# Dilated attention: q and k sorted by class for each dilation, v single-buffered and reloaded by dilation, 16 staging slots

## The chip, the cores and the metric

The kernel runs on one core of a Trainium2 chip. The metric is the device time of a run in microseconds (us); smaller is better.

## What is computed

The program is a transformer block of 2048 tokens and width 1024 with two kinds of attention, followed by a second, sliding-window block. The change lies in one stage alone, the dilated attention of the first block: 8 heads of 64, each token attending in a radius of 64 positions at three dilations. Cut from the reference:

```python
DIL_HEADS = 8
DIL_PATTERNS = ((128, 1), (512, 4), (2048, 16))
...
def dilated_branch(q, k, v, slopes, window, dilation):
    r = window // (2 * dilation)
    ...
    qs = split(q)              # positions split into residue classes
    kw = window3(split(k))     # each block of r with its two neighbours
    vw = window3(split(v))
    ...
    s = jnp.einsum('bnqche,bnkche->bnchqk', qs, kw).astype(jnp.float32) * scale + bias
    s = jnp.where(mask, s, MASK_VALUE)
    m = jnp.max(s, axis=-1, keepdims=True)
    e = jnp.exp(s - m)
    l = jnp.sum(e, axis=-1, keepdims=True)
    o = jnp.einsum('bnchqk,bnkche->bnqche', e.astype(v.dtype), vw)
```

For dilation d the tokens t with equal t mod d form a class; within it the pattern is a plain band of radius 64. The three outputs are merged in a later stage by their softmax sums.

## The kernel before

`build` runs seven stages one after the other: an input projection (names with p_), a global attention (d_), the dilated attention (l_), a merge with a projection (m_), a gated embedding (g_), a second projection (s_), and windowed attention with its projection (w_). Each stage is a `Phase`: it owns its buffers and semaphores, its engines meet at a barrier at the end, and then GpSimd clears the stage's semaphores one by one (L78) before its own work in the next stage.

`dilated_attention` treats 4 pairs of heads. A pair is 24 steps, 8 for each of the dilations 1, 4 and 16, in this order (a dilation is called a level below); a step is two units, a unit 128 queries of one class for the two heads of the pair. Step n on each engine:

- TensorE, `scores`: two bias matmuls (L1110) and then twelve of 64x128 weights (q) and 64x256 keys (L1123), in three passes over the high and low parts of q and k. q and k lie in token order, so at dilation d both operands are read with a distance of d elements: `q_part[own, par, start:start + d * (P - 1) + 1:d]`. At dilation 16 a window holds the whole class and half of the scores are used. Then `transposes` (L1134) of the step before and `values` (L1149) of the one before that, unit by unit; at dilation 16 these are half as many.
- VectorE, `top`: the row maxima (L1071), one TENSOR_REDUCE a step, written into the staging ring; then `move` (L1079, three of four units) and `move_out` (L1084, the outputs into the ring).
- ScalarE, `exp` (L1009), and `move` for every fourth unit (L1018).
- SyncE (SP), the DMA queue, in program order: it waits until a step is staged and issues its two stores (L956). The ring `stage` has 8 slots, so `top` of step n waits until the stores of step n - 4 have landed. At step 2 and 4 of a pair it loads q and k of the next pair into `raw` (L919), at step 6 all of its v, in front of step 6's stores: `if at == 6: load_v(pair + 1)`, 16 DMAs (L933 to L940) into the other half of the double buffer `v`, once in the order of each dilation, 3 MB in all.
- GpSimd: at the start an iota, the zero edges of k and the masks (L976); then for each next pair the high part (L990) and the low part (L992) of q and k.

At the stage's start VectorE zeroes the edges of v (L1035, L1036, 20 memsets), makes distances (L1039, L1043), ScalarE and VectorE split q and k of the first pair, GpSimd cuts the masks out of the distances, and VectorE copies them into `tables` (L1057, L1059), which the first bias matmul needs.

Of the kernel before, what the change touches and what calls it, by code (L numbers as in the profile page):

```python
# [16 lines left out]
ALU = mybir.AluOpType  # L17
ACT = mybir.ActivationFunctionType
F32 = mybir.dt.float32
# [808 lines left out]
def dilated_attention(nc, c, cols, rows, o_parts):  # L828
# [32 lines left out]
    with Phase(nc, "l") as ph:  # L861
        ident = c["ident"]
        raw = ph.sb("raw", [P, 2, S])
        q_hi = ph.sb("q_hi", [P, 2, S], F32R)
        q_lo = ph.sb("q_lo", [P, 2, S], F32R)
        k_hi = ph.sb("k_hi", [P, 2, S + 2 * PAD], F32R)
        k_lo = ph.sb("k_lo", [P, 2, S + 2 * PAD], F32R)
        v = ph.sb("v", [P, 2, CHUNKS, 2 * HD])
# [5 lines left out]
        stage = ph.sb("stage", [P, 8, PAIR_OUT])  # L874
# [5 lines left out]
        v_loaded = ph.sems("v_loaded", 2)  # L880
# [3 lines left out]
        parts_made = ph.sem("parts_made")  # L884
        counted = ph.sem("counted")
# [13 lines left out]
        stored = ph.sems("stored", 8)  # L899
# [15 lines left out]
        def _(sp):  # L915
# [5 lines left out]
            def load_v(pair):  # L921
                if pair >= 2:
                    sp.wait_ge(valued, 2 * SPP * (pair - 1))
                if pair == 0:
                    sp.wait_ge(v_padded, 20)
                at = BV * P + pair * 2 * HD
                src, dst, arrived = rows[:, at:at + 2 * HD], v[:, pair % 2], v_loaded[pair % 2]
                chunk = 0
                for d in (1, 4):
                    tiles = NT // d  # L930
                    for cls in range(d):
                        own = src.rearrange("(i d) n -> d i n", d=d)[cls]
                        sp.dma_start(dst[REACH:P, chunk], own[0:REACH, :]).then_inc(arrived, 16)  # L933
                        sp.dma_start(dst[:, chunk + 1:chunk + tiles],
                                     own[REACH:REACH + (tiles - 1) * P, :].rearrange("(j p) n -> p j n", p=P))\
                          .then_inc(arrived, 16)
                        sp.dma_start(dst[0:REACH, chunk + tiles], own[tiles * P - REACH:tiles * P, :])\
                          .then_inc(arrived, 16)
                        chunk += tiles + 1
                sp.dma_start(dst[:, chunk:chunk + NT], src.rearrange("(i d) n -> i d n", d=NT)).then_inc(arrived, 16)  # L940
# [1323 lines left out]
```

## Time and profile before

| | us |
|---|---|
| median of 3 runs | 3359.24 |
| lowest, highest | 3358.46, 3363.28 |
| the profiled execution's own time | 3359.32 |
| its span, first to last instruction | 3357.2 |
| TensorE busy in the span | 3115.7 (93%) |
| VectorE busy | 1657.7 (49%) |
| ScalarE busy | 1227.4 (37%) |
| GpSimd busy | 454.0 (14%) |

The busy times are means over seven stages with different limits; what the change is worth is read from the l_ stage alone. A row of a trace gives start, duration, engine, line, operation and buffers, and in brackets how long the engine was idle before it and what ended the idle time. Start times are counted from the span's start.

### The profile page before, as it was taken

The page shows a single profiled execution, that of the slowest core. Times are in us where ns is not written, and L with a number is a line of the kernel's source. Part 1 is how long each engine was busy: PE and PEld are TensorE (multiplying, and loading weights), DVE is VectorE, ACT ScalarE, POOL GpSimd, SP SyncE. Part 2 cuts the span into 40 slices and gives each one's busy share as a digit, 9 for nine tenths or more (in the row PEclk, how much of TensorE's full clock was granted, in tenths as well). Part 3 has the DMA queues.
Part 4 walks back from the last instruction along what each step waited for, and adds up shares of the span by engine and source line. Part 5 has one row for each costly group of instructions (what it writes and reads, how often), then busy time and mean ns, then how long its engine had stood idle before and what let it go on. Part 6 is the DMA issues. An engine that isn't in the chain of part 4 may idle for free. (4 is left out here: it accounts for less than half of the span.)

```text
span 3357.2 us, 49168 instructions
## 1 busy us (share of the span) xinstructions
PE 3115.7 (93%) x19138; PEld 2656.3 (79%) x19138; DVE 1657.7 (49%) x2855; ACT 1227.4 (37%) x2695; POOL 454.0 (14%) x249
## 2 busy tenths in 40 slices
PE   7999999997999999879999599699689999799998
PEld 7877778985788888768888478588588888699997
DVE  4466664002888888745445477333341100166664
ACT  3222221011677777635445211222231111254543
POOL 1110110111102101021010344200101100121111
PEclk9999999998999999979899799899899999799999
DMA  5111212223101111042131466422234431444342
GB/s 170 60 66 56 68 61 66 72 63 90 25 22 51 33 33 28 33 120 79 48 92 33 147 225 228 139 73 83 107 121 111 115 100 53 149 141 131 119 127 76
DMA packets 254561, 303.01 MB, mean 90 GB/s; under 512 B 18768, under 2 KB 201088, under 8 KB 251136
## 3 DMA queue, kind: packets, MB, share of 16 engines
q1 hardware_dynamic: 254336, 299.92, 28.7%
q8 instruction: 152, 2.49, 0.3%
q14 instruction: 73, 0.60, 0.1%
HBM read 190.38 MB, written 109.47 MB: 89 GB/s over the span
## 5 line engine op out<-in xcount | busy, mean ns | idle before, releaser
L708 DVE CUSTOM_DVE_ANT_0 d_e<-d_score,d_dist,d_slope 128x1024 f32<-128x1024 f32 x256 | 318.5, 1281 | 64.5 <-PE d_score L764 64.4
L477 PE MATMUL p_acc<-p_h_hi,p_w_hi 128*128 128x512 f32 x768 | 324.2, 422 | 1.0 <-issue 1.0
L477 PE MATMUL p_acc<-p_h_hi,p_w_lo 128*128 128x512 f32 x768 | 300.0, 391 | 0.0
L477 PE MATMUL p_acc<-p_h_lo,p_w_hi 128*128 128x512 f32 x768 | 299.4, 390 | 0.0
L420 DVE RECIPROCAL p_root<-p_root 128x512 f32<-128x512 f32 x64 | 214.6, 3353 | 149.9 <-ACT p_root L344 149.9
L642 ACT ACTIVATE d_e<-d_e,d_neg_top 128x2048 f32<-128x2048 f32 x128 | 257.1, 2008 | 84.8 <-DVE d_neg_top L717 84.6
L787 PE MATMUL d_out<-d_v,d_w_t 128*128 128x128 f32 x2048 | 252.2, 277 | 0.0
L787 PEld LDWEIGHTS d_out<-d_v,d_w_t 128*128 128x128 f32 x2048 | 241.5, 194 | 0.0
L477 PE MATMUL s_acc<-s_h_hi,s_w_hi 128*128 128x512 f32 x576 | 224.4, 390 | 0.0
L477 PE MATMUL s_acc<-s_h_lo,s_w_hi 128*128 128x512 f32 x576 | 224.1, 389 | 0.0
L477 PE MATMUL s_acc<-s_h_hi,s_w_lo 128*128 128x512 f32 x576 | 224.1, 389 | 0.0
L1009 ACT ACTIVATE l_e<-l_score,l_stage 128x256 f32<-128x256 f32 (+1 forms) x384 | 163.3, 437 | 160.1 <-DVE l_stage L1071 157.8
L1071 DVE TENSOR_REDUCE l_stage<-l_score 128x4 f32<-128x1024 f32 (+1 forms) x96 | 100.5, 1047 | 160.0 <-PE l_score L1123 135.8
L477 PEld LDWEIGHTS p_acc<-p_h_hi,p_w_hi 128*128 128x128 f32 x768 | 144.2, 188 | 43.9 <-issue 16.2
L477 PEld LDWEIGHTS p_acc<-p_h_lo,p_w_hi 128*128 128x128 f32 x768 | 144.2, 188 | 43.3 <-issue 14.9
L1149 PE MATMUL l_out<-l_v,l_e_t 128*128 128x64 f32 x1280 | 170.6, 274 | 0.0
L477 PEld LDWEIGHTS p_acc<-p_h_hi,p_w_lo 128*128 128x128 f32 x768 | 144.2, 188 | 30.6
L649 ACT ACTIVATE d_w_t<-d_turn 128x512 f32<-128x512 f32 x256 | 138.9, 597 | 74.8 <-PE d_turn L774 74.8
L1149 PEld LDWEIGHTS l_out<-l_v,l_e_t 128*128 128x128 f32 x1280 | 165.4, 199 | 0.0
L309 POOL TENSOR_TENSOR p_w_lo<-p_w_raw,p_w_hi 128x2048 fp32r<-128x2048 f32 x16 | 73.3, 4584 | 650.6 <-ACT p_w_hi L337 650.6
L732 DVE SCALAR_TENSOR_TENSOR d_e<-d_e,d_ratio 128x2048 f32<-128x2048 f32 x64 | 159.5, 2492 | 0.0
L470 PE MATMUL p_acc<-p_w_hi,p_h_hi 128*128 128x256 f32 x512 | 147.4, 288 | 11.5 <-DVE p_h_lo L390 11.5
(258 smaller groups left out, 6961.4 us busy)
## 6 DMA issues: line engine op xcount, KB each, us to landing
p_w_raw<-in_w_in SPq DMA_DIRECT2D x16, 1024.0 KB, 6.7
cols<-p_stage SPq DMA_DIRECT2D x64, 256.0 KB, 2.3
q<-s_parts SPq DMA_DIRECT2D x128, 128.0 KB, 2.4
w_q<-q SPq DMA_DIRECT2D x16, 1024.0 KB, 8.8
o_parts<-l_stage SPq DMA_DIRECT2D x192, 66.0 KB, 1.7
m_o<-o_parts SPq DMA_DIRECT2D x48, 264.0 KB, 4.9
s_w_raw<-in_a_w_in SPq DMA_DIRECT2D x10, 1024.0 KB, 5.4
rows<-p_stage SPq DMA_DIRECT2D x32, 256.0 KB, 2.1
```

Source lines behind the costliest of these rows:

```text
L309: pool.tensor_tensor(w_lo[:, i % 2], w_raw[:, i % 2], w_hi[:, i % 2].bitcast(F32), ALU.subtract).then_inc(w_lo_made, 1)
L420: dve.reciprocal(root[:, m % 2], root[:, m % 2]).then_inc(root_inverted, 1)
L470: mm = pe.matmul(acc[:, room, two * BLK:(two + 1) * BLK], h_part[:, kt, at], w_part[:, j, kt], start=(kt == 0 and m == 0), stop=(kt == KT ...
L477: mm = pe.matmul(acc[:, room], w_part[:, j, kt, ct * P:(ct + 1) * P], h_part[:, kt, tc * BANK:(tc + 1) * BANK], start=(kt == 0 and m == 0) ...
L642: act.activation(e[:, m % 3, s], e[:, m % 3, s], ACT.Exp, bias=neg_top[:, m % 2, s:s + 1], accum_out=sums).then_inc(exped, 1)
L649: act.activation(w_t[:, m % 2, 4 * r:4 * r + 4], turn[:, r % 2].rearrange("p (b n) -> p b n", n=P), ACT.Copy).then_inc(moved, 1)
L708: dve.tensor_tensor_reduce(e[:, m % 3, s, half * HALF:(half + 1) * HALF], score[:, 2 * half:2 * half + 2].rearrange("p a b -> p (a b)"), d ...
L732: dve.scalar_tensor_tensor(out=e[:, m % 3, 0], in0=e[:, m % 3, 1], scalar=ratio[:, m % 2, 1:2], in1=e[:, m % 3, 0], op0=ALU.mult, op1=ALU. ...
L787: mm = pe.matmul(out[:, m % 2, 0:VW], w_t[:, m % 2, kt], v[:, h % 2, kt], start=(kt == 0), stop=(kt == NT - 1))
L1009: act.activation(e[:, u % 4, h, 0:width(n)], score[:, 2 * (n % 2) + h, scores_of(n, j)], ACT.Exp, bias=stage[:, u % 8, 2 * HD + h:2 * HD + ...
L1071: dve.tensor_reduce(stage[:, 2 * n % 8:2 * n % 8 + 2, 2 * HD:2 * HD + 2], own, AX_X, ALU.max, negate=True)\
L1149: mm = pe.matmul(out[:, n % 2, (2 * j + h) * HD:(2 * j + h + 1) * HD], e_t[:, u % 4, w * h + k], v[:, pair % 2, chunk + k, h * HD:(h + 1) ...
```

## The change

- q and k are kept three times, once for each level, in buffers q_hi1, q_hi4, q_hi16 and so on, each sorted by class, so that all operands of the scores are contiguous. The buffers are single: there is no half for the next pair. The split on GpSimd (or, for the first pair, on ScalarE and VectorE) fills level 1; GpSimd then copies it into the order of level 4 and of level 16, four copies each (`sort_parts`), reading with a distance of 4 or 16 elements. A level's buffers are refilled when the pair before has made its last scores of that level.
- v is single as well, with a buffer for each level (v1, v4, v16). Its 16 loads for the next pair are spread over steps 9 to 11 (v1), 16 to 23 and, in the next pair, 0 to 3 (v4), and 4 (v16), one a step, behind the step's stores. The values wait for v once a level instead of once a pair.
- The staging ring has 16 slots. The stage has 11 semaphores more: `stored` 16 instead of 8, `v_loaded` 3 instead of 2, and two `sorted_made`.
- The loads of raw q and k stand behind the stores of their step. VectorE zeroes 10 edges of v instead of 20; GpSimd's zero edges of k are 8 memsets instead of 4, of fewer elements.

```diff
     STEPS = dilated_steps()
     SPP = len(STEPS)
     TOTAL = PAIRS * SPP
-    PAD = REACH * 4
     WIN = 2 * P
-    CHUNKS = (NT + 1) + 4 * (NT // 4 + 1) + NT
-    V_DMAS = 3 + 4 * 3 + 1
+    LEVELS = len(DILATIONS)
+    SPL = SPP // LEVELS
+    KEYS = (S + 2 * REACH, S + 4 * 2 * REACH, S)
+    CHUNKS = (NT + 1, 4 * (NT // 4 + 1), NT)
+    V_DMAS = (3, 12, 1)
     KINDS = 6
+    SLOTS = 16
+
+    def level_of(n):
+
+        return n % SPP // SPL
+
+    def whole(tensor, d):
+
+        return tensor.rearrange("p (i c) -> p c i", c=d)
+
+    def classes(tensor, d):
+
+        return tensor.rearrange("p (c i) -> p c i", c=d)
+
+    def inner(keys, d):
+
+        return classes(keys, d)[:, :, REACH:REACH + S // d] if d < NT else classes(keys, d)
...
-        q_hi = ph.sb("q_hi", [P, 2, S], F32R)
-        q_lo = ph.sb("q_lo", [P, 2, S], F32R)
-        k_hi = ph.sb("k_hi", [P, 2, S + 2 * PAD], F32R)
-        k_lo = ph.sb("k_lo", [P, 2, S + 2 * PAD], F32R)
-        v = ph.sb("v", [P, 2, CHUNKS, 2 * HD])
+        q_hi = [ph.sb(f"q_hi{d}", [P, S], F32R) for d in DILATIONS]
+        q_lo = [ph.sb(f"q_lo{d}", [P, S], F32R) for d in DILATIONS]
+        k_hi = [ph.sb(f"k_hi{d}", [P, n], F32R) for d, n in zip(DILATIONS, KEYS)]
+        k_lo = [ph.sb(f"k_lo{d}", [P, n], F32R) for d, n in zip(DILATIONS, KEYS)]
+        v = [ph.sb(f"v{d}", [P, n, 2 * HD]) for d, n in zip(DILATIONS, CHUNKS)]
...
-        stage = ph.sb("stage", [P, 8, PAIR_OUT])
+        stage = ph.sb("stage", [P, SLOTS, PAIR_OUT])
...
-            def load_v(pair):
-                if pair >= 2:
-                    sp.wait_ge(valued, 2 * SPP * (pair - 1))
-                if pair == 0:
-                    sp.wait_ge(v_padded, 20)
+            def load_v(pair, level, part):
...
+                if pair >= 1:
+                    sp.wait_ge(valued, 2 * (SPP * (pair - 1) + SPL * (level + 1)))
...
-                sp.dma_start(dst[:, chunk:chunk + NT], src.rearrange("(i d) n -> i d n", d=NT)).then_inc(arrived, 16)
+                src, dst, arrived = rows[:, at:at + 2 * HD], v[level], v_loaded[level]
+                if d == NT:
+                    sp.dma_start(dst[:, :], src.rearrange("(i d) n -> i d n", d=NT)).then_inc(arrived, 16)
+                    return
+                own = src.rearrange("(i d) n -> d i n", d=d)[cls]
+                chunk = cls * (tiles + 1)
+                if part % 3 == 0:
+                    sp.dma_start(dst[REACH:P, chunk], own[0:REACH, :]).then_inc(arrived, 16)
+                elif part % 3 == 1:
+                    sp.dma_start(dst[:, chunk + 1:chunk + tiles],
+                                 own[REACH:REACH + (tiles - 1) * P, :].rearrange("(j p) n -> p j n", p=P))\
+                      .then_inc(arrived, 16)
+                else:
+                    sp.dma_start(dst[0:REACH, chunk + tiles], own[tiles * P - REACH:tiles * P, :])\
+                      .then_inc(arrived, 16)
 
             for item in range(2):
                 load_raw(0, item)
-            load_v(0)
+            sp.wait_ge(v_padded, 10)
+            for level in range(LEVELS):
+                for part in range(V_DMAS[level]):
+                    load_v(0, level, part)
...
-                if pair + 1 < PAIRS:
-                    if at in (2, 4):
-                        load_raw(pair + 1, at // 2 - 1)
-                    if at == 6:
-                        load_v(pair + 1)
                 sp.wait_ge(staged, n + 1)
...
-                    sp.dma_start(own[b * P:(b + 1) * P, :], stage[:, u % 8]).then_inc(stored[u % 8], 16)
-            for s in range(8):
-                sp.wait_ge(stored[s], 16 * 2 * TOTAL // 8)
+                    sp.dma_start(own[b * P:(b + 1) * P, :], stage[:, u % SLOTS]).then_inc(stored[u % SLOTS], 16)
+                if pair + 1 < PAIRS:
+                    if at in (2, 4):
+                        load_raw(pair + 1, at // 2 - 1)
+                    if SPL + 1 <= at < SPL + 4:
+                        load_v(pair + 1, 0, at - SPL - 1)
+                    if at >= 2 * SPL:
+                        load_v(pair + 1, 1, at - 2 * SPL)
+                if pair >= 1:
+                    if at < 4:
+                        load_v(pair, 1, SPL + at)
+                    if at == 4:
+                        load_v(pair, 2, 0)
...
-            for part in (k_hi, k_lo):
-                for edge in (slice(0, PAD), slice(PAD + S, S + 2 * PAD)):
-                    pool.memset(part[:, :, edge].bitcast(F32), 0.0).then_inc(padded, 1)
+            for level, d in enumerate(DILATIONS[:2]):
+                for part in (k_hi[level], k_lo[level]):
+                    length = S // d + REACH
+                    for edge in (slice(0, REACH), slice(length, length + REACH)):
+                        pool.memset(classes(part, d)[:, :, edge].bitcast(F32), 0.0).then_inc(padded, 1)
...
+            def sort_parts(pair, level):
+                d = DILATIONS[level]
+                pool.wait_ge(parts_made, 2 * pair + 2)
+                if pair >= 1:
+                    pool.wait_ge(scored, SPP * (pair - 1) + SPL * (level + 1))
+                for part, out_part in ((q_hi, classes(q_hi[level], d)), (q_lo, classes(q_lo[level], d)),
+                                       (k_hi, inner(k_hi[level], d)), (k_lo, inner(k_lo[level], d))):
+                    own = part[0][:, :] if part in (q_hi, q_lo) else part[0][:, REACH:REACH + S]
+                    pool.tensor_copy(out_part, whole(own, d)).then_inc(sorted_made[level - 1], 1)
+
+            for pair in range(PAIRS):
+                if pair >= 1:
+                    for item, (hi, lo) in enumerate(((q_hi[0][:, :], q_lo[0][:, :]),
+                                                     (k_hi[0][:, REACH:REACH + S], k_lo[0][:, REACH:REACH + S]))):
+                        pool.wait_ge(raw_loaded[item], 16 * (pair + 1))
+                        pool.wait_ge(sorted_made[1], 4 * pair)
+                        pool.wait_ge(scored, SPP * (pair - 1) + SPL)
+                        pool.tensor_copy(hi, raw[:, item]).then_inc(hi_made, 1)
+                        pool.wait_ge(hi_made, 2 * pair + item + 1)
+                        pool.tensor_tensor(lo, raw[:, item], hi.bitcast(F32), ALU.subtract).then_inc(parts_made, 1)
+                for level in (1, 2):
+                    sort_parts(pair, level)
 
...
-                hi = (q_hi[:, 0], k_hi[:, 0, PAD:PAD + S])[item]
-                lo = (q_lo[:, 0], k_lo[:, 0, PAD:PAD + S])[item]
+                hi = (q_hi[0][:, :], k_hi[0][:, REACH:REACH + S])[item]
+                lo = (q_lo[0][:, :], k_lo[0][:, REACH:REACH + S])[item]
...
             def scores(n):
-                pair = n // SPP
-                par, banks = pair % 2, 2 * (n % 2)
+                pair, level, banks = n // SPP, level_of(n), 2 * (n % 2)
                 if n % SPP == 0:
                     pe.wait_ge(parts_made, 2 * pair + 2)
+                elif n % SPL == 0:
+                    pe.wait_ge(sorted_made[level - 1], 4 * pair + 4)
...
                     for j, (d, cls, b, _) in enumerate(step_of(n)):
-                        start = cls + d * P * b
+                        length = S // d + (2 * REACH if d < NT else 0)
                         for h in range(2):
                             own = slice(h * HD, (h + 1) * HD)
-                            q = q_part[own, par, start:start + d * (P - 1) + 1:d]
-                            if d == NT:
-                                keys = k_part[own, par, PAD:PAD + S].rearrange("p (k c) -> p c k", c=NT)\
-                                    [:, cls // 2 * 2:cls // 2 * 2 + 2]
-                            else:
-                                at = PAD + start - d * REACH
-                                keys = k_part[own, par, at:at + d * (WIN - 1) + 1:d]
+                            q = q_part[level][own, cls * (S // d) + b * P:cls * (S // d) + (b + 1) * P]
+                            at = cls * length + b * P if d < NT else cls // 2 * WIN
+                            keys = k_part[level][own, at:at + WIN]
...
+                if n % SPL == 0 and j == 0:
+                    pe.wait_ge(v_loaded[level], 16 * V_DMAS[level] * (pair + 1))
                 wait_moved(pe, u)
...
+                                       v[level][:, chunk + k, h * HD:(h + 1) * HD], start=(k == 0), stop=(k == w - 1))
                 mm.then_inc(valued, 1)
```

Where rows move on the queues and engines, word for word from the listed programs. SyncE first, from the last load of the first pair's v on (L956 or L976 are the stores, L919 or L939 raw q and k, the l_v rows the loads of v). Before:

```order
L940 DMA l_v<-rows 128x16x128
L956 DMA o_parts<-l_stage 128x132 x4
L919 DMA l_raw<-cols 128x2048
L956 DMA o_parts<-l_stage 128x132 x4
L919 DMA l_raw<-cols 128x2048
L956 DMA o_parts<-l_stage 128x132 x4
L933 DMA l_v<-rows 64x128
L934 DMA l_v<-rows 128x15x128
L937 DMA l_v<-rows 64x128
L933 DMA l_v<-rows 64x128
L934 DMA l_v<-rows 128x3x128
L937 DMA l_v<-rows 64x128
```

The change, from the same place:

```order
L950 DMA l_v<-rows 128x16x128
L976 DMA o_parts<-l_stage 128x132 x6
L939 DMA l_raw<-cols 128x2048
L976 DMA o_parts<-l_stage 128x132 x4
L939 DMA l_raw<-cols 128x2048
L976 DMA o_parts<-l_stage 128x132 x10
L955 DMA l_v<-rows 64x128
L976 DMA o_parts<-l_stage 128x132 x2
L957 DMA l_v<-rows 128x15x128
L976 DMA o_parts<-l_stage 128x132 x2
L961 DMA l_v<-rows 64x128
L976 DMA o_parts<-l_stage 128x132 x10
```

Before, the loads of v follow each other without a store between them (10 more rows of them follow); now two stores stand between any two of them.

GpSimd at the start of the stage, with what each row waits for. Before:

```order
L966 MEMSET l_k_hi 128x2x256 x2
L966 MEMSET l_k_lo 128x2x256 x2
L976 AFFINE_SELECT l_plain<-l_plain 128x256 [waits l_distance]
L976 AFFINE_SELECT l_plain<-l_plain 128x256 [waits l_masked] x17
L990 CAST l_q_hi<-l_raw 128x2048 [waits l_raw_loaded0,l_masked]
L992 TENSOR_TENSOR l_q_lo<-l_raw,l_q_hi 128x2048 [waits l_hi_made]
```

The change, from the masks on:

```order
L1010 AFFINE_SELECT l_plain<-l_plain 128x256 [waits l_masked] x17
L1025 COPY l_q_hi<-l_q_hi 128x2048 [waits l_parts_made,l_masked]
L1025 COPY l_q_lo<-l_q_lo 128x2048
L1025 COPY l_k_hi<-l_k_hi 128x4x512
L1025 COPY l_k_lo<-l_k_lo 128x4x512
L1025 COPY l_q_hi<-l_q_hi 128x2048 [waits l_parts_made]
L1025 COPY l_q_lo<-l_q_lo 128x2048
L1025 COPY l_k_hi<-l_k_hi 128x2048
L1025 COPY l_k_lo<-l_k_lo 128x2048
L1034 CAST l_q_hi<-l_raw 128x2048 [waits l_scored,l_sorted_made1,l_raw_loaded0]
```

The eight sorting copies of the first pair have come in directly behind the masks, and the next pair's split waits for them and for the first eight steps' scores.

GpSimd at the end of the stage (L78 are the clears of semaphores, L1394 or L1437 its first work in the next stage). Before:

```order
L55 UNCONDITIONAL_BRANCH
L78 ISA x30
L1377 UNCONDITIONAL_BRANCH
L1394 MEMSET m_half_down 128x1
L1395 TENSOR_TENSOR m_root<-k_a_sums 128x64
```

The change:

```order
L55 UNCONDITIONAL_BRANCH
L78 ISA x41
L1420 UNCONDITIONAL_BRANCH
L1437 MEMSET m_half_down 128x1
L1438 TENSOR_TENSOR m_root<-k_a_sums 128x64
```

Eleven clears more stand ahead of the next stage's first row.


## Rows read from the trace of the kernel before

**Rows 1.** The page, its first line.

```profile
span 3357.2 us, 49168 instructions
```

**Rows 2.** Timeline of VectorE: start, duration, row maxima L1071, idle time before.

```profile
1554.32 1.23 DVE L1071 TENSOR_REDUCE l_stage<-l_score 128x4 f32<-128x1024 f32 x1 [1.01 <-PE l_score L1123]
...
1665.24 1.23 DVE L1071 TENSOR_REDUCE l_stage<-l_score 128x4 f32<-128x1024 f32 x1 [1.01 <-PE l_score L1123]
...
1772.91 1.22 DVE L1071 TENSOR_REDUCE l_stage<-l_score 128x4 f32<-128x1024 f32 x1 [1.01 <-PE l_score L1123]
...
1775.72 1.23 DVE L1071 TENSOR_REDUCE l_stage<-l_score 128x4 f32<-128x1024 f32 x1 [0.59 <-PE l_score L1123]
...
1795.51 1.22 DVE L1071 TENSOR_REDUCE l_stage<-l_score 128x4 f32<-128x1024 f32 x1 [1.01 <-PE l_score L1123]
...
1799.65 1.23 DVE L1071 TENSOR_REDUCE l_stage<-l_score 128x4 f32<-128x1024 f32 x1 [1.01 <-PE l_score L1123]
...
1804.59 1.23 DVE L1071 TENSOR_REDUCE l_stage<-l_score 128x4 f32<-128x1024 f32 x1 [1.82 <-PE l_score L1123]
...
1867.26 0.69 DVE L1071 TENSOR_REDUCE l_stage<-l_score 128x4 f32<-128x512 f32 x1 [1.74 <-PE l_score L1123]
...
1870.74 0.69 DVE L1071 TENSOR_REDUCE l_stage<-l_score 128x4 f32<-128x512 f32 x1 [1.68 <-PE l_score L1123]
```

**Rows 3.** The same timeline in the first pair, steps 9, 10 and 13.

```profile
1483.59 1.23 DVE L1071 TENSOR_REDUCE l_stage<-l_score 128x4 f32<-128x1024 f32 x1 [1.82 <-PE l_score L1123]
...
1494.43 1.22 DVE L1071 TENSOR_REDUCE l_stage<-l_score 128x4 f32<-128x1024 f32 x1 [7.71 <-DMA o_parts<-l_stage]
...
1510.13 1.23 DVE L1071 TENSOR_REDUCE l_stage<-l_score 128x4 f32<-128x1024 f32 x1 [1.82 <-PE l_score L1123]
```

**Rows 4.** Windows: length, busy PE, PEld, DVE, ACT, POOL; clock, DMA, GB/s.

```profile
1457.02:1473.57 16.55, 16.55 (x155) 14.55 (x153) 10.56 (x14) 8.93 (x34) 6.45 (x2) 1.00 0.48 150
...
1488.00:1512.00 24.00, 20.69 (x139) 18.33 (x135) 9.17 (x13) 7.50 (x29) 0.00 (x0) 0.79 0.31 82
```

**Rows 5.** Line L1123, ns min/median/max, in dilation 1 and in dilation 4.

```profile
L1123 PEld LDWEIGHTS l_score<-l_k_lo,l_q_hi x14: 183/185/188, 1460.5 to 1472.9; 64*128 64x128 f32 x14
...
L1123 PEld LDWEIGHTS l_score<-l_k_lo,l_q_hi x20: 329/332/333, 1813.1 to 1833.2; 64*128 64x128 f32 x20
```

**Rows 6.** Timeline of SyncE's queue: the first v load and the next store.

```profile
1477.97 0.46 SPq L933 DMA_DIRECT2D l_v<-rows  x1
...
1488.44 80.01 SPq L956 DMA_DIRECT2D o_parts<-l_stage  x40
```

**Rows 7.** Timeline of GpSimd: the copy of 2048 elements.

```profile
1466.99 1.90 POOL L990 CAST l_q_hi<-l_raw 128x2048 fp32r<-128x2048 f32 x1 [25.01 <-DMA l_raw<-cols]
```

**Rows 8.** Timeline of the stage's start.

```profile
1420.58 0.17 DVE L1035 MEMSET l_v<- 64x128 f32 x1 [14.42 <-PEq L55]
...
1422.71 0.34 POOL L962 IOTA l_e<- 128x256 f32 x1 [83.31 <-issue]
...
1425.48 0.42 DVE L1039 SCALAR_TENSOR_TENSOR l_e<-l_e 128x256 f32<-128x256 f32 x1
...
1427.59 14.39 POOL L976 TENSOR_SCALAR_AFFINE_SELECT l_plain<-l_plain 128x256 f32<-128x256 f32 x18 [2.68 <-DVE l_plain L1043]
...
1442.02 2.11 DVE L1057 CAST l_tables<-l_plain 128x256 fp32r<-128x256 f32 x10 [8.42 <-POOL l_plain L976]
...
1444.55 1.19 PE L1110 MATMUL l_score<-l_tables,l_slopes 128*128 128x512 f32 x2 [26.67 <-DVE l_tables L1059]
```

**Rows 9.** Line L976, the masks: ns min/median/max.

```profile
L976 POOL TENSOR_SCALAR_AFFINE_SELECT l_plain<-l_plain x18: 398/398/2536, 1427.6 to 1441.6; 128x256 f32<-128x256 f32 x18
```

**Rows 10.** Timeline of the next stage's start.

```profile
1877.85 0.34 SPq L1328 DMA_DIRECT2D m_bucket_values<-in_t_table  x1
...
1879.98 0.10 POOL L1394 MEMSET m_half_down<- 128x1 f32 x1 [179.86 <-issue]
...
1892.33 0.69 DVE L1479 TENSOR_TENSOR m_ya<-m_a,m_root 128x512 f32<-128x512 f32 x1 [1.83 <-POOL m_root L1403]
```

More of the change, by code:

```diff
@@ L981, in _ @@
             assert steps == 18
-            for pair in range(1, PAIRS):
-                par = pair % 2
-                for item, (hi, lo) in enumerate(((q_hi[:, par], q_lo[:, par]),
-                                                 (k_hi[:, par, PAD:PAD + S], k_lo[:, par, PAD:PAD + S]))):
-                    pool.wait_ge(raw_loaded[item], 16 * (pair + 1))
-                    if pair >= 2:
-                        pool.wait_ge(scored, SPP * (pair - 1))
-                    pool.tensor_copy(hi, raw[:, item]).then_inc(hi_made, 1)
-                    pool.wait_ge(hi_made, 2 * pair + item + 1)
-                    pool.tensor_tensor(lo, raw[:, item], hi.bitcast(F32), ALU.subtract).then_inc(parts_made, 1)
+            def sort_parts(pair, level):
+                d = DILATIONS[level]
+                pool.wait_ge(parts_made, 2 * pair + 2)
[17 more added lines that the diff above has]
+                    sort_parts(pair, level)
         @block.scalar
@@ L1070, in top @@
                     own = own.rearrange("p h (u n) -> p u h n", u=2)
-                dve.tensor_reduce(stage[:, 2 * n % 8:2 * n % 8 + 2, 2 * HD:2 * HD + 2], own, AX_X, ALU.max, negate=True)\
+                dve.tensor_reduce(stage[:, 2 * n % SLOTS:2 * n % SLOTS + 2, 2 * HD:2 * HD + 2], own, AX_X, ALU.max, negate=True)\
                    .then_inc(top_made, 1)
@@ L1139, in values @@
                 n, j = u // 2, u % 2
-                pair, chunk = n // SPP, step_of(n)[j][3]
+                pair, level = n // SPP, level_of(n)
+                d, cls, b, _ = step_of(n)[j]
+                chunk = cls * (NT // d + 1) + b if d < NT else cls
                 w = width(n) // P
-                if n % SPP == 0 and j == 0:
-                    pe.wait_ge(v_loaded[pair % 2], 16 * V_DMAS * (pair // 2 + 1))
+                if n % SPL == 0 and j == 0:
+                    pe.wait_ge(v_loaded[level], 16 * V_DMAS[level] * (pair + 1))
                 wait_moved(pe, u)
@@ L1149, in values @@
                         mm = pe.matmul(out[:, n % 2, (2 * j + h) * HD:(2 * j + h + 1) * HD], e_t[:, u % 4, w * h + k],
-                                       v[:, pair % 2, chunk + k, h * HD:(h + 1) * HD], start=(k == 0), stop=(k == w - 1))
+                                       v[level][:, chunk + k, h * HD:(h + 1) * HD], start=(k == 0), stop=(k == w - 1))
                 mm.then_inc(valued, 1)
```

46 lines of the change are left out of this document (18 added, 28 removed).

## The prediction

> **What bounds it now.** The execution that I take apart spans 3357.2 us [rows 1]. I went straight to the stage that the diff touches, whose engines' activity runs from about 1420 to 1877 us, and asked which engine sets its pace. The windows give it: in an undisturbed stretch of dilation 1, TensorE is busy 16.55 of 16.55 us at full granted clock, VectorE 10.56 and ScalarE 8.93 [rows 4]. So a step costs what its matmuls cost, and the start times of the reductions at L1071, one for each step, are a clock for the loop. The reader is to see in [rows 2], where the last pair of heads runs without disturbance: 4.14 us from one step to the next at dilation 1 (1795.51 to 1799.65), 4.94 at dilation 4 (1799.65 to 1804.59), 3.48 at dilation 16 (1867.26 to 1870.74), and 2.81 in the first step after a pair boundary (1772.91 to 1775.72), where the transposes and values are still the narrow ones of dilation 16 but the scores are already dilation 1. In every one of these rows VectorE waited for L1123, so TensorE was the later one.
>
> The loop also has one hole in each of the first three pairs. At 1494.43 the reduction waited 7.71 us for a store of the staging ring [rows 3]. The wait row names the DMA; why it was late stands on the sync queue: the loads of the next pair's v begin to be issued at 1477.97, and the next store is issued at 1488.44 [rows 6], 10.5 us later, and lands behind them. With 8 slots (4 steps) the ring runs dry. Afterwards the granted clock of the stretch is 0.79 [rows 4], so the hole costs more than the wait.
>
> **Term 1, contiguous scores.** Number and shapes of the matmuls stay. The weight loads of the scores take 185 ns at dilation 1 and 332 at dilation 4 [rows 5], with the same 64x128 form; what differs is that q and keys are read at a distance of 4 elements. The change reads all three levels contiguously, so I price dilation 4 at the row of dilation 1: 4.94 - 4.14 = 0.80 us a step. For dilation 16 the row with contiguous scores and narrow rest is the 2.81 of [rows 2]: 3.48 - 2.81 = 0.67. Eight steps of each in 4 pairs: 32 x 0.80 + 32 x 0.67 = 47.0 us. Below that lies nothing unless VectorE takes over: in the narrow step it had 1.68 us idle before its reduction [rows 2], more than the 0.67 taken out. A rule of the Trainium skill goes with this row (SBUF — State Buffer, Door 1: lines of 16 bytes, so fp32 strides of 4 elements hit a new line each time); it gives no price.
>
> **Term 2, the hole.** A pair without loads costs 1870.74 - 1772.91 = 97.83 for 23 steps, plus 2.81 for the step across the boundary: 100.64. The pairs that start at 1554.32 and 1665.24 take 110.92 and 107.67 [rows 2]: 10.28 and 7.03 too many. In the first pair four steps take 1510.13 - 1483.59 = 26.54 [rows 3] against 4 x 4.94 = 19.76: 6.78. Sum 24.1 us. After the change each step's stores go out before at most one or two loads, and 16 slots let a store be 8 steps late, 22 us even in the shortest steps. The densest place is steps 2 to 4 of a pair: raw q, raw k, the last loads of v4 and the whole v16, just over 3 MB. The old burst of 3 MB kept its store back by 10.5 us of issue and to 1494.43 in all, 16.5 us from 1477.97; the new one has the issue apart and steps of 4.14 us (33 us for 8). So the hole goes whole: 24.1, bounds 0 and 24.1. v4 is complete at step 3 and first used by the values of step 8, v16 at step 4 for step 16.
>
> **Term 3, sorting on GpSimd.** Eight copies of 128x2048 for each pair, strided on the read side. No row shows one. Below: the contiguous CAST of that size, 1.90 us; above: the two-input subtraction that follows it, 6.45 us of both less 1.90 = 4.55 us [rows 4, 7]. I stretch the CAST by what striding does to the weight loads, 332/185: 3.4 us, and keep both ends. Cover: in the first pair the copies follow the masks, from about 1442, and the scores of step 8 need four of them at about 1474, so up to 8.0 us a copy hides; later pairs give 16 steps (over 50 us) for each group of four, and the whole GpSimd load of a pair is 8 x 3.4 + 2 x (1.90 + 4.55) = 40 us of about 89. VectorE and TensorE keep their pace while GpSimd works today: the stretch of 16.55 us has 6.45 us of it [rows 4]. Price 0. The skill's GPSIMD Engine Reference (Performance pitfalls) speaks against this: 2.9 cycles an element when the read step is over 8 bytes; at its 1.2 GHz that is an estimate of 4.95 us a copy. By row or by rule the sum is the same, since 8.0 is the point where it begins to matter.
>
> **Term 4, the start.** TensorE waits 26.67 us for the tables, at the end of this chain: VectorE's 20 memsets of v from 1420.58 to the next instruction at 1425.48, 0.245 us each, then distance, masks, tables [rows 8]. Ten memsets go: 1423.03. The iota on which the next instruction also waits ends at 1422.71 + 0.34 = 1423.05, so little more than that could be had. GpSimd's memsets become 8 smaller ones, less elements in all, finished before the masks can start [rows 8]. Gain 2.3 us; bounds 0 and 2.5.
>
> **Term 5, semaphores.** 11 more are cleared by GpSimd behind the stage. Today it is released with SyncE at 1877.85 and does its first work at 1879.98 after 30 clears: 0.071 each, so 0.8 us [rows 10]. This is on the path: the next stage's VectorE waits 1.83 us for GpSimd at 1892.33 [rows 10]. Loss 0.8.
>
> **Sum.** 47.0 + 24.1 + 2.3 - 0.8 = 72.6 us off the profiled execution's 3359.3 (its span 3357.2 and 2.1 around it): 3286.7. The median of the runs is 3359.24, the same. 0.2% is 6.7 us, about what a measurement tells from no change.
>
> **Rivals.**
> *The start collides.* One mask took 2.536 us instead of the usual 0.398 [rows 9], while VectorE was also at work on the same memory: something of the two engines is shared. After the change both want to go at the end of the masks: VectorE with its 12 table copies, GpSimd with its sorting. Today the masks end at 1427.59 + 14.39 = 1441.98 and VectorE starts at 1442.02 [rows 8], 0.04 us later, while GpSimd would first pass a wait of its own for the last mask; so VectorE should be first and hold GpSimd off for some 2.4 us, which is hidden. If GpSimd is first, TensorE starts one copy later, 1.9 to 4.55 us: 3289 to 3291; if the copies go in turn with the table copies, up to eight of them, 36 us: 3323. This is how the skill states it (SBUF — State Buffer, Who interferes with whom): the engine that starts first has the shared pair for the whole instruction and the other blocks. Chance 0.08.
> *The stores stay late.* Moving 3 MB in three steps, or v4 trickling in between stores, still empties the ring, now elsewhere. All of term 2 lost: 3311. The half of it: 3299. Against it: 16 slots against a delay that was 16.5 us. Chance 0.06.
> *Stride is not the price.* Then the steps stay at 4.94 and 3.48, and only the rest comes: 3334. The forms in [rows 5] are equal but for the stride, so 0.02.
> *GpSimd becomes the bound: slower.* If a strided copy costs above 8.0 us, the levels of the first pair wait; later a pair lasts 12.9 + 8X instead of 89, and the whole gain of 72.6 is eaten at 4 x (12.9 + 8X - 89) = 72.6, X = 11.8 us; at X = 13 the time is 3359 + 4 x 8 x 1.2 = 3398. That is 2.6 times the dearest row of this size. Chance 0.05, of which 0.02 ends faster, 0.01 the same, 0.02 slower.
>
> **Numbers.** The forecast has the rest, 0.79, and its own range 3282 to 3292 (start 0 to 2.5, the moment at which TensorE's clock rises at the stage's start, about 1 us either way, a small rest of the hole). The range to hold 8 in 10 takes in one copy at the start and half of term 2 above, and a step that falls a little under the 2.81 below: 3278 to 3298. Faster 0.97, same 0.01, slower 0.02.
>
> **What would show it.** Term 1: reductions 4.14 us apart in all of dilation 4 and 2.8 in dilation 16, weight loads of L1123's successor at 185 ns everywhere. Term 2: no reduction that waits for a store, granted clock 1.00 from the first pair's start to the last. Term 3: sorting copies of 2 to 5 us on GpSimd, and no step at a level's start later than its neighbours. Term 4: the first matmul of the stage near 1442.2. Term 5: a gap of 2.9 us on GpSimd where 2.13 stands now. It is wrong if a level's first scores wait for GpSimd, if table copies on VectorE last microseconds, or if VectorE's reduction stops waiting for TensorE in the narrow steps, which would mean that its own chain is the longer one there.

## The result, and the profile after

| | before | changed |
|---|---|---|
| median of the runs, us | 3358.85 (4 runs) | 3311.78 (4 runs, 3308.67 to 3317.32) |
| ratio to before, 95% interval | | 0.9862, 0.9843 to 0.9881 |
| span of the profiled execution, us | 3357.2 | 3306.8 |

The kernel became 47 us faster, not 72.6: below the forecast gain and outside the range of 3278 to 3298. That is 1.4% where 2.2% was forecast: with 2% as the least that is called faster it counts as the same, to which the forecast gave a chance of 0.01, although the interval lies clear of 1. The stage's loop came out as forecast; its start did not.

VectorE's timeline of the changed kernel, with the row maxima, answers to [rows 2]: start, duration, idle time before. The last pair again:

```profile
1732.35 1.23 DVE L1115 TENSOR_REDUCE l_stage<-l_score 128x4 f32<-128x1024 f32 x1 [1.01 <-PE l_score L1164]
...
1788.05 1.22 DVE L1115 TENSOR_REDUCE l_stage<-l_score 128x4 f32<-128x1024 f32 x1 [1.01 <-PE l_score L1164]
...
1792.18 1.23 DVE L1115 TENSOR_REDUCE l_stage<-l_score 128x4 f32<-128x1024 f32 x1 [1.01 <-PE l_score L1164]
...
1815.38 0.69 DVE L1115 TENSOR_REDUCE l_stage<-l_score 128x4 f32<-128x512 f32 x1 [1.01 <-PE l_score L1164]
...
1818.19 0.69 DVE L1115 TENSOR_REDUCE l_stage<-l_score 128x4 f32<-128x512 f32 x1 [1.01 <-PE l_score L1164]
```

Steps are 4.13 us apart at dilation 4 and 2.81 at dilation 16; the pair's 23 steps take 85.84 instead of 97.83. TensorE's granted clock is 0.99 from 1476 to 1830, where [rows 4] had 0.79 behind the first hole. The waits of VectorE from 1466 to 1826 name no DMA any more (who waited for whom: total, times, longest):

```profile
DVE l_stage L1115 <- PE l_score L1164: 97.3, 96, 3.0
DVE l_e_t L1123 <- PE l_turn L1175: 27.6, 53, 0.7
DVE l_stage L1128 <- PE l_out L1192: 2.1, 5, 0.5
```

The timeline of the stage's start, which answers to [rows 8], shows where the gain went:

```profile
1413.89 0.17 DVE L1080 MEMSET l_v<- 64x128 f32 x1 [14.43 <-PEq L55]
...
1419.22 14.39 POOL L1010 TENSOR_SCALAR_AFFINE_SELECT l_plain<-l_plain 128x256 f32<-128x256 f32 x18 [1.50 <-DVE l_plain L1087]
...
1433.64 30.18 DVE L1101 CAST l_tables<-l_plain 128x256 fp32r<-128x256 f32 x10 [7.33 <-POOL l_plain L1010]
1463.75 0.35 DVE L1103 CAST l_tables<-l_plain 128x128 fp32r<-128x128 f32 x2
...
1464.24 1.19 PE L1155 MATMUL l_score<-l_tables,l_slopes 128*128 128x512 f32 x2 [53.05 <-DVE l_tables L1103]
```

Ten table copies that took 2.11 us take 30.18, and TensorE's wait for the tables grows from 26.67 us [rows 8] to 53.05. GpSimd's timeline in the same stretch:

```profile
1433.67 3.92 POOL L1025 CAST l_q_hi<-l_q_hi 128x2048 fp32r<-128x2048 f32 x1
1437.54 3.87 POOL L1025 CAST l_q_lo<-l_q_lo 128x2048 fp32r<-128x2048 f32 x1
...
1459.81 3.66 POOL L1025 CAST l_k_lo<-l_k_lo 128x2048 fp32r<-128x2048 f32 x1
```

and the table copies by themselves, ns min/median/max:

```profile
L1101 DVE CAST l_tables<-l_plain x10: 280/3684/3901, 1433.6 to 1463.5; 128x256 fp32r<-128x256 f32 x10
```

The median copy of 256 elements is as long as a sorting copy of 2048. The ledger of the stage, from its first memset to GpSimd's first work in the next one (1879.98 in [rows 10], 1828.17 after):

| part, us | before | after | difference | forecast |
|---|---|---|---|---|
| first memset to first matmul | 23.97 | 50.35 | +26.4 | -2.3 |
| first matmul to last row maximum | 426.19 | 353.95 | -72.2 | -71.1 |
| last row maximum to the next stage | 9.24 | 9.98 | +0.7 | +0.8 |
| stage | 459.4 | 414.3 | -45.1 | -72.6 |

The rest of the span differs by 5.3 us between these two executions, in stages that the diff doesn't touch: the stage's start itself lies at 1410 to 1421 us in the executions below. So the experiments are read by the stage's own parts first. A time given below without a ratio is that of a single run; single runs of the kernel before lay between 3347 and 3364 us in this series.

### The profile page after: what moved, and what is told of

Read it like the earlier page. It is cut to its first block and busy times, and to the rows that moved or that the text cites. A ratio compares the mean times of both kernels' runs of the same rounds, so it can differ in the third digit from the quotient of the medians.

```text
span 3306.8 us, 49221 instructions
## 1 busy us (share of the span) xinstructions
PE 3052.2 (92%) x19138; PEld 2599.0 (79%) x19138; DVE 1684.9 (51%) x2845; ACT 1227.1 (37%) x2695; POOL 573.6 (17%) x285
## 5 line engine op out<-in xcount | busy, mean ns | idle before, releaser
L1192 PE MATMUL l_out<-l_v,l_e_t 128*128 128x64 f32 x1280 | 163.8, 267 | 0.0
L1192 PEld LDWEIGHTS l_out<-l_v,l_e_t 128*128 128x128 f32 x1280 | 157.9, 192 | 0.0
L774 PEld LDWEIGHTS d_turn<-k_ident,d_e 128*128 128x128 f32 x1024 | 110.4, 141 | 56.3 <-DVE d_e L732 33.9
```

What stands on the lines that cost most here:

```text
L774: mm = pe.transpose(turn[:, r % 2, b * P:(b + 1) * P], e[:, m % 3, 0, (4 * r + b) * P:(4 * r + b + 1) * P], ident[:, :])
L1192: mm = pe.matmul(out[:, n % 2, (2 * j + h) * HD:(2 * j + h + 1) * HD], e_t[:, u % 4, w * h + k], v[level][:, chunk + k, h * HD:(h + 1) * H ...
```

## The experiments

### Sorting after the tables

```diff
+            pool.wait_ge(tables_made, 2 * KINDS)
             for pair in range(PAIRS):
```

> The changed kernel, but GpSimd begins to sort only when all 12 table copies are made. Theory 1 (hand-over: each of VectorE's table copies has to wait for one whole sorting copy of GpSimd, so eight copies of 3.7 to 3.9 us stand in front of the tables): the table copies are done 2.4 us after the masks, TensorE's first wait in the stage is some 24 us instead of 53.1, the steps stay at 4.14 and 2.81, and the time is the changed kernel's 3311.8 less 28 to 29: 3283 to 3284. The sorted parts of dilation 4 are then ready 16 us after the tables, step 8 needs them after 30, so no new wait. Theory 2 (TensorE's start waits for the sorting itself or for something else that is late in this execution): 3312, with the same 53 us of wait.

Measured 3281.21 us, ratio 0.9782 (0.9757 to 0.9808). VectorE's and TensorE's timeline:

```profile
1410.05 0.17 DVE L1081 MEMSET l_v<- 64x128 f32 x1 [14.43 <-PEq L55]
...
1429.26 2.11 DVE L1102 CAST l_tables<-l_plain 128x256 fp32r<-128x256 f32 x10 [6.79 <-POOL l_plain L1010]
...
1431.79 1.19 PE L1156 MATMUL l_score<-l_tables,l_slopes 128*128 128x512 f32 x2 [24.45 <-DVE l_tables L1104]
```

The first matmul comes 21.74 us after the first memset, 28.6 us earlier than in the changed kernel, and the ten copies take 2.11 us again. The row maxima span 351.0 us, as in the changed kernel, and still wait for TensorE alone 96 times, 97.3 us in total in both, so the later sorting makes no level wait. The stage is 1795.60 - 1410.05 = 385.6 us: 73.8 less than before, where 72.6 were forecast. Theory 1 (each table copy waits for a whole sorting copy) holds and theory 2 falls.

### Tables by another form of instruction

```diff
-                    dve.tensor_copy(tables[:, kind, j * WIN:(j + 1) * WIN], plain[:, n])...
+                    dve.tensor_reduce(tables[:, kind, j * WIN:(j + 1) * WIN], plain[:, n].unsqueeze(2), AX_X, ALU.max)...
...
```

> The changed kernel with the same order of work, but VectorE makes the tables by a TENSOR_REDUCE over an axis of one element instead of a copy: same bytes in and out, one source, another form of instruction. Theory 1a (only the copy form shares something exclusive with GpSimd): each of the 12 takes 0.3 to 0.4 us while GpSimd's 3.9 us copies run beside it, TensorE's first wait is 24 to 26 us, the time 3283 to 3286. Theory 1b (any access of VectorE to this memory is held up by GpSimd's strided reading): each takes 3.7 to 3.9 us as now, and the time stays at 3312.

The last two copies are changed likewise. Measured 3283.71, and TensorE's first wait 25.73 us. The timeline of both engines:

```profile
1433.24 3.36 DVE L1101 TENSOR_REDUCE l_tables<-l_plain 128x256 fp32r<-128x256 f32 x10 [6.79 <-POOL l_plain L1010]
1433.27 3.84 POOL L1025 CAST l_q_hi<-l_q_hi 128x2048 fp32r<-128x2048 f32 x1
1436.52 0.47 DVE L1104 TENSOR_REDUCE l_tables<-l_plain 128x128 fp32r<-128x128 f32 x2
```

Twelve instructions pass beside one sorting copy, none of them held up (the longest lasts 0.42 us) and the sorting copy as short as ever. So what stops VectorE isn't the access to the memory (SBUF, the on-chip buffer) but the form: a CAST from SBUF to SBUF shares something exclusive with GpSimd, a TENSOR_REDUCE of the same bytes doesn't. This agrees with the Trainium skill (SBUF — State Buffer, Who interferes with whom), which lists copies and casts, and not reductions, among what takes the shared pair of ports. The reduction is the slower form: 3.36 us for ten, where ten casts with nothing beside them take 2.11.

### Half copies

```diff
-                    pool.tensor_copy(out_part, whole(own, d)).then_inc(sorted_made[level - 1], 1)
+                    if pair == 0:
+                        pool.tensor_copy(out_part[:, 0:d // 2], whole(own, d)[:, 0:d // 2])
+                        pool.tensor_copy(out_part[:, d // 2:d], whole(own, d)[:, d // 2:d])\
+                            .then_inc(sorted_made[level - 1], 1)
+                    else:
+                        pool.tensor_copy(out_part, whole(own, d)).then_inc(sorted_made[level - 1], 1)
```

> The changed kernel, with each of the first pair's eight sorting copies cut in two of half the size (about 1.95 us each). Theory 1 (one for one: after each copy of GpSimd VectorE gets in one of its own): VectorE's 12 copies meet 11 half copies, so the tables come after about 11 x 1.95 = 21 us instead of 30, TensorE's first wait is 44 to 45 us, the time 3303. Theory 3 (GpSimd's list of work runs to its end and VectorE is only let in at gaps that have nothing to do with single instructions): the tables come when all sorting is over, 53 us of wait as now, 3312.

Measured 3305.38, and TensorE's first wait 43.68 us. VectorE's timeline and line L1106 of this kernel:

```profile
1440.45 18.15 DVE L1106 CAST l_tables<-l_plain 128x256 fp32r<-128x256 f32 x10 [6.28 <-POOL l_plain L1010]
1458.52 3.77 DVE L1108 CAST l_tables<-l_plain 128x128 fp32r<-128x128 f32 x2
```

```profile
L1106 DVE CAST l_tables<-l_plain x10: 295/2072/2081, 1440.4 to 1456.6; 128x256 fp32r<-128x256 f32 x10
```

The twelve copies are over after 21.8 us; all but the first last one half copy. They take turns one for one, as theory 1 says, and are done while half copies are still to come; theory 3 falls.

### Copies without the sorting

```diff
-                    pool.tensor_copy(out_part, whole(own, d)).then_inc(sorted_made[level - 1], 1)
+                    pool.tensor_copy(out_part, classes(own, d)).then_inc(sorted_made[level - 1], 1)
```

> The changed kernel with the eight copies a pair, but reading contiguously, so q and k of dilations 4 and 16 are not in the order of the classes (the scores are of wrong tokens; sizes and counts are kept). Theory 1: copies take 1.9 us (the contiguous cast of the same size takes 1.89), the loss at the start is 8 x 1.9 = 15 us instead of 30, TensorE's first wait 39 us, the time 3298; the steps stay at 4.14 and 2.81. If the loss at the start doesn't scale with the length of a copy, theory 1 falls.

Measured 3301.48, TensorE's first wait 38.05 us. GpSimd's copies are the short ones here (line L1025, ns min/median/max), against 3655 to 3939 for those of the changed kernel:

```profile
L1025 POOL CAST l_q_hi<-l_q_hi x8: 1891/1898/2010, 1439.0 to 1720.4; 128x2048 fp32r<-128x2048 f32 x8
```

From first memset to first matmul 35.35 us, 13.6 more than with the tables first; eight copies of 1.9 are 15.2, less the 8 x 0.2 that the table copies take anyway: 13.6. The same sum for the changed kernel: four of 3.85 and four of 3.65, 30.0 less 1.6 = 28.4, measured 28.6. So here the loss is the length of GpSimd's copies times their number, up to the number of table copies.

### Sorting in the middle of the tables

```diff
+            pool.wait_ge(tables_made, 3)
             for pair in range(PAIRS):
```

> The changed kernel, but GpSimd's sorting begins when 3 of the 12 table copies are made, so it comes in the middle of VectorE's row of copies. Theory P (what the prediction counted on: a row of VectorE's copies that is already running keeps GpSimd out to its end, and only the very first copy was too short a lead): no table copy is longer than 0.3 us, from the first memset to TensorE's first matmul 21.7 us as in a1_tables_first, time 3281 to 3284. Theory H (the memory is handed over at the end of every instruction for which the other engine waits, whatever stands behind it): the table copies left, about 7 to 8, each wait for one sorting copy, 7 x 3.8 = 26 us less their own 0.2 each, so 46 to 48 us to the first matmul and 3307 to 3309.

Measured 3313.14; first memset at 1420.65. VectorE's and TensorE's timeline, and the line of the table copies:

```profile
1439.63 19.95 DVE L1102 CAST l_tables<-l_plain 128x256 fp32r<-128x256 f32 x10 [6.28 <-POOL l_plain L1010]
1459.51 7.19 DVE L1104 CAST l_tables<-l_plain 128x128 fp32r<-128x128 f32 x2
...
1466.85 1.19 PE L1156 MATMUL l_score<-l_tables,l_slopes 128*128 128x512 f32 x2 [48.90 <-DVE l_tables L1104]
```

```profile
L1102 DVE CAST l_tables<-l_plain x10: 285/1998/3889, 1439.6 to 1455.9; 128x256 fp32r<-128x256 f32 x10
```

46.2 us to the first matmul, as theory H forecast; the time, a single run's, is 4 us above its 3309, outside this part. The five copies before GpSimd's arrival last 0.29 us, the seven behind it 3.6 to 3.9 each. A row of copies in progress keeps nobody out: theory H (handed over at the end of every instruction) holds, and my reading P falls.

### Tables on ScalarE

```diff
+            for kind, halves in enumerate(((1, 0), (0, 0), (0, 2), (4, 3), (3, 5))):
+                act.wait_ge(masked, (5, 5, 8, 13, 16)[kind])
+                for j, n in enumerate(halves):
+                    act.activation(tables[:, kind, j * WIN:(j + 1) * WIN], plain[:, n], ACT.Copy)\
+                       .then_inc(tables_made, 1)
+            act.wait_ge(masked, 18)
...
-            dve.wait_ge(masked, 18)
...
-                    dve.tensor_copy(tables[:, kind, j * WIN:(j + 1) * WIN], plain[:, n]).then_inc(tables_made, 1)
...
```

> The changed kernel, but ScalarE makes the tables, each as soon as its masks are cut, and VectorE does nothing at that place; GpSimd sorts directly behind the masks. Theory 1 (the loss lies between VectorE's copies and GpSimd only, ScalarE doesn't share with GpSimd): ScalarE's copies take 0.3 to 0.45 us beside GpSimd's 3.8 us copies, the last two come right after the last mask instead of twelve, so the first matmul is about 1.5 us earlier than in a1_tables_first: some 20 us after the stage's first memset, time 3280 to 3283, ratio to the kernel before 0.976 to 0.978. Rival (any second engine is held up by the sorting): ScalarE's last copies take 3.7 us each and the first matmul comes 27 to 50 us after the memset.

Measured 3283.59, ratio 0.9782 (0.9765 to 0.9799). The timeline of ScalarE, GpSimd and TensorE:

```profile
1438.54 0.51 ACT L1057 ACTIVATE l_tables<-l_plain 128x128 fp32r<-128x128 f32 x2 [0.36 <-POOL l_plain L1010]
1438.57 3.87 POOL L1025 CAST l_q_hi<-l_q_hi 128x2048 fp32r<-128x2048 f32 x1
...
1439.19 1.19 PE L1159 MATMUL l_score<-l_tables,l_slopes 128*128 128x512 f32 x2 [22.31 <-ACT l_tables L1057]
```

ScalarE's last two copies, 0.29 and 0.31 us long, run beside a sorting copy of 3.87 us and don't wait for it. First memset at 1419.59, so 19.6 us to the first matmul, 2.1 less than with the tables first, and the stage is 384.3 us, 1.3 less. In the medians that can't be told: both kernels have the ratio 0.9782. Either is 0.8% faster than the changed kernel, and the simpler edit is the one wait.

### The ring alone, and the spread loads alone

The kernel before with 16 slots, and the kernel with the tables first with 8 (the first edit also takes 16 for 8 wherever the ring's slots and semaphores are counted):

```diff
-        stage = ph.sb("stage", [P, 8, PAIR_OUT])
+        stage = ph.sb("stage", [P, 16, PAIR_OUT])
...
```

```diff
-    SLOTS = 16
+    SLOTS = 8
```

> The kernel before with one edit: 16 staging slots instead of 8. Theory (the ring is what runs dry): the loads of v still keep the stores back by 16.5 us, 16 slots give 8 steps of 4.9 us or 39 us, so the reduction never waits for a store and the 24.1 us of the hole go: 3335, steps at 4.94 and 3.48 as before. Rival (the burst itself slows the stage, by the queue or the memory): a part of the 24 us stays with 16 slots too, 3340 to 3359.

> The kernel with the tables first (a1_tables_first), but 8 staging slots: loads of v spread, ring as before. Theory (spreading alone is enough): at steps 2 to 4 of a pair about 3 MB are issued within 8 to 12 us, stores wait behind at most 1 to 2 MB, 4 to 7 us, and 8 slots give 4 steps of 4.14 or 16 us: no wait for a store, the time that of a1_tables_first, 3284. Rival (the slots were needed): a wait of the reduction for o_parts at steps 5 to 8 of each pair, some 2 to 8 us each, 3290 to 3308.

The first measured 3326.76. Its row maxima, at the line that [rows 2] come from (first and last start after the durations), with who kept them waiting:

```profile
L1071 DVE TENSOR_REDUCE l_stage<-l_score x96: 691/1225/1226, 1441.3 to 1840.4; 128x4 f32<-128x1024 f32 x64, 128x4 f32<-128x512 f32 x32
...
  PE l_score L1123: 144.9, 96
```

399.1 us instead of 423.3: the ring alone takes the whole hole away, 24.2, with the burst of loads still there, and no reduction waits for a DMA. (That the run is 8 us below my 3335 lies outside these parts; the stage is 23.7 shorter.) The second measured 3287.37, and here I missed:

```profile
L1116 DVE TENSOR_REDUCE l_stage<-l_score x96: 691/1224/1226, 1446.0 to 1798.5; 128x4 f32<-128x1024 f32 x64, 128x4 f32<-128x512 f32 x32
...
  PE l_score L1165: 89.5, 89
  DMA o_parts<-l_stage: 11.4, 6
```

Six reductions wait for a store, the longest 3.3 us of idle time where 1.0 is usual, but the stretch is only 1.5 us longer (352.5) than the 351.0 of the kernel with 16 slots: most of what a late store delays is made up in the next step (behind the longest wait, steps of 6.47 and 2.07 us where 4.14 each is usual). The theory's "no wait" was wrong, its time nearly right. So either part is nearly enough by itself: 16 slots with the burst, or the spread loads with 8.

### One operand contiguous

The kernel before, with q or the keys read contiguously at all dilations and the other strided as before:

```diff
-                            q = q_part[own, par, start:start + d * (P - 1) + 1:d]
+                            q = q_part[own, par, (cls * (S // d) + b * P):(cls * (S // d) + b * P) + P]
```

```diff
-                                at = PAD + start - d * REACH
-                                keys = k_part[own, par, at:at + d * (WIN - 1) + 1:d]
+                            at = PAD - REACH + cls * (S // d) + b * P
+                            keys = k_part[own, par, at:at + WIN]
```

> The kernel before, but TensorE reads q (the weights) contiguously at all dilations, keys strided as before; the scores of dilations 4 and 16 are thus of wrong queries, counts and sizes are kept. Theory W (strided weight loads alone are the price): steps at dilation 4 fall from 4.94 to 4.14, at dilation 16 from 3.48 to 2.81, 47 us of the stage. Theory K (the strided keys are): steps stay at 4.94 and 3.48. If both cost, a step lies between, and with b4 the parts add up to 0.80 or more.

> The kernel before, but TensorE reads the keys contiguously at all dilations, q strided as before; scores of dilations 4 and 16 are of wrong keys, counts and sizes are kept. Theory W: steps stay at 4.94 and 3.48. Theory K: 4.14 and 2.81. If the slower of the two reads hides the other (they run beside each other), both this kernel and b3 stay close to 4.94, and only both together give 4.14.

They measured 3357.91 and 3350.46; both leave out the order of the classes at dilations 4 and 16 and keep sizes and counts. The last pair, which no load disturbs, tells them apart. VectorE's timeline with q contiguous:

```profile
1775.14 1.23 DVE L1071 TENSOR_REDUCE l_stage<-l_score 128x4 f32<-128x1024 f32 x1 [1.01 <-PE l_score L1123]
...
1816.29 1.23 DVE L1071 TENSOR_REDUCE l_stage<-l_score 128x4 f32<-128x1024 f32 x1 [1.67 <-PE l_score L1123]
...
1821.09 1.23 DVE L1071 TENSOR_REDUCE l_stage<-l_score 128x4 f32<-128x1024 f32 x1 [1.67 <-PE l_score L1123]
...
1867.59 0.69 DVE L1071 TENSOR_REDUCE l_stage<-l_score 128x4 f32<-128x512 f32 x1 [1.58 <-PE l_score L1123]
...
1870.98 0.69 DVE L1071 TENSOR_REDUCE l_stage<-l_score 128x4 f32<-128x512 f32 x1 [1.59 <-PE l_score L1123]
```

and with the keys contiguous:

```profile
1769.86 1.23 DVE L1071 TENSOR_REDUCE l_stage<-l_score 128x4 f32<-128x1024 f32 x1 [1.01 <-PE l_score L1119]
...
1820.79 1.23 DVE L1071 TENSOR_REDUCE l_stage<-l_score 128x4 f32<-128x1024 f32 x1 [1.71 <-PE l_score L1119]
...
1825.63 1.23 DVE L1071 TENSOR_REDUCE l_stage<-l_score 128x4 f32<-128x1024 f32 x1 [1.71 <-PE l_score L1119]
...
1862.91 0.69 DVE L1071 TENSOR_REDUCE l_stage<-l_score 128x4 f32<-128x512 f32 x1 [1.64 <-PE l_score L1119]
...
1866.34 0.69 DVE L1071 TENSOR_REDUCE l_stage<-l_score 128x4 f32<-128x512 f32 x1 [1.63 <-PE l_score L1119]
```

| last pair | 23 steps, us | dilation 4 | dilation 16 |
|---|---|---|---|
| both strided | 97.83 | 4.95 | 3.48 |
| q contiguous | 95.84 | 4.80 | 3.39 |
| keys contiguous | 96.48 | 4.84 | 3.43 |
| both contiguous (changed) | 85.84 | 4.14 | 2.81 |

With q contiguous its weight loads are short again, 205 ns instead of 332:

```profile
L1123 PEld LDWEIGHTS l_score<-l_k_lo,l_q_hi x20: 205/205/206, 1814.9 to 1834.4; 64*128 64x128 f32 x20
```

and the step is still 4.80. Neither theory W nor K: 2.0 us and 1.4 us alone, 12.0 together, which is the third outcome that the second expectation names. It fits a pace set by the slower of two reads that run beside each other; that this is the mechanism is my reading, which no run isolates. Over the whole stage neither kernel gains anything: 459.5 and 460.2 us against 459.4. Their first three pairs, where the ring still runs dry, take 2 us more than before instead of 6 and 4 less; why the holes grew is open. The row on which I priced term 1 (the weight loads' 185 against 332) would by itself have been the wrong one; the price held because I took it from whole steps.

## Why the prediction was wrong

- **Term 1, contiguous scores: right.** 12.0 us in the last pair against the 11.8 that eight steps of 0.80 and eight of 0.67 make, and 399.1 - 351.1 = 48.0 us from the kernel before with 16 slots to the changed one, against 47.0; VectorE had 1.01 us to spare even in the shortest step.
- **Term 2, the hole: right in size** (together with term 1 the loop lost 72.2 us against 71.1). The ring alone gives 24.2 of it; the spreading adds nothing that these runs can tell, with 16 slots in place.
- **Term 3, sorting: the length near, the price of 0 wrong, and this is the step that failed.** A strided copy takes 3.66 to 3.94 us where I had 3.4, far from the 8.0 at which the levels would wait, and no level did. (The 4.95 us that I estimated from the Trainium skill's GPSIMD Engine Reference, Performance pitfalls for Q7 kernels, is above what these copies took.) But the prediction put the copies' cost at nothing because of cover in TensorE's schedule, and dealt with VectorE's table copies in a rival alone: VectorE is first at the end of the masks "and hold GpSimd off for some 2.4 us". VectorE was first, by 0.03 us, and it didn't matter: the shared resource went to GpSimd after one table copy, back after one sorting copy, and so on eight times. Table copies that last microseconds are the very sign of being wrong that the prediction had named. The rival with copies in turn, written at 3323 and sharing a chance of 0.08 with the milder form of the collision, is what happened; with the copies at 3.4 us that the forecast itself used it would have read 3286.7 + 8 x 3.4 = 3314, and 3311.8 was measured. The sum of these runs' numbers: 28.6 us at the start, which the tables first give back.
- **Why I chose wrongly.** [Rows 9] give only the least, the median and the greatest duration of a mask. The prediction speaks of one long mask and reads it as GpSimd being held off for as long as VectorE has work. The timeline of the kernel before, in two adjoining windows, has more:

```profile
1428.92 2.54 POOL L976 TENSOR_SCALAR_AFFINE_SELECT l_plain<-l_plain 128x256 f32<-128x256 f32 x1
1428.97 2.23 DVE L1052 TENSOR_TENSOR l_q_lo<-l_raw,l_q_hi 128x2048 fp32r<-128x2048 f32 x1
...
1431.12 2.48 DVE L1052 TENSOR_TENSOR l_k_lo<-l_raw,l_k_hi 128x2048 fp32r<-128x2048 f32 x1
...
1431.60 2.26 POOL L976 TENSOR_SCALAR_AFFINE_SELECT l_plain<-l_plain 128x256 f32<-128x256 f32 x1
```

  Two masks are long, one beside each of VectorE's two subtractions, and the first is over at 1431.46, 0.34 us after the second subtraction has begun, which takes 2.48 us instead of 2.23. That fits turns, one for one: GpSimd was let in between two instructions of VectorE. So the turn by turn that the prediction priced, and then left out on the strength of who comes first, could be seen before any run. The kernel that sorts behind three tables settles it: a lead of five copies protects none of the rest. The second point stood in the same rows: the masks' end is the one place in this stage where VectorE copies from SBUF to SBUF on the path, twelve times, and where a long list of GpSimd's work was now to begin.
- **Term 4, the start: right, once freed.** 21.7 us instead of 24.0 with the tables first: 2.2 gained against 2.3.
- **Term 5, semaphores: right.** 0.7 us against 0.8 (GpSimd's first work comes 2.91 us after SyncE's, at 1825.26 and 1828.17; 2.13 before).

With the start mended, the stage's gain is 73.8 us where the forecast had 72.6, and the median 3281.2 lies inside the range.

## What to carry to other kernels

Before GpSimd is given long instructions, look for every stretch in which VectorE copies between buffers in SBUF: as these runs show it for casts, each such copy can cost one whole GpSimd instruction, so the bill is the smaller count times the GpSimd instruction's length, not the length of the shorter work, and being first saves only the copies that are over by then. A wait that puts the short list ahead, another form of instruction or another engine each took the loss away here. Where a strided matmul is made contiguous, both operands have to be: one of them alone gave a tenth to a sixth of the gain in an undisturbed pair and none over the stage, so price such an edit by whole steps in a stretch where both reads are contiguous. A ring that runs dry may need only slots: moving the loads that caused it was not required here, and with the loads moved 8 slots were nearly enough.

## What the runs showed of the hardware that I had not expected

- CASTs on VectorE from SBUF to SBUF and GpSimd's CASTs alternate one for one, also into a row of copies that is already running (a table copy of 0.29 us becomes 3.6 to 3.9, or 1.97 and 2.07 with GpSimd instructions of 1.9 and 2.06); TENSOR_REDUCE from SBUF (0.41 us for 128x256), and ScalarE's copies (0.29 and 0.31 us for 128x128), aren't held up. VectorE's TENSOR_TENSOR of two SBUF inputs stretches a mask on GpSimd too, from 0.40 us to 2.54 and 2.26.
- GpSimd's copy of 128x2048 takes 1.9 us contiguous, about 3.9 reading every 4th element and 3.66 to 3.74 reading every 16th, when the output is contiguous: twice the time, and not more for the larger distance.
- TensorE's weight loads at distance 16 aren't slower than at distance 4 either: 307 ns against 332 in the kernel before.
